# Seven normalisations of a two-block transformer kernel: statistics with tokens on partitions instead of tokens on columns

## The chip, the cores and the metric

The kernel runs on one core of one Trainium2 chip. TensorE (PE) multiplies matrices, VectorE (DVE) and ScalarE (ACT) do the elementwise work, and the DMA queues bring the weights. The metric is the device time of one execution in microseconds (us); shorter is better. The kernel before has a median of 2540.64 us over three runs (2532.92 to 2546.59).

## The reference, cut to what matters

Two blocks follow one another, each of two layers, on 256 tokens of width 1024 (the first block carries 256 context tokens beside them, so 512 columns up to its second layer). In front of and behind every mixer and feed-forward stage stands a norm. The first block has RMS norms, the second has layer norms:

```python
def rmsnorm(x, g):
    xf = x.astype(jnp.float32)
    y = xf * lax.rsqrt(jnp.mean(xf * xf, axis=-1, keepdims=True) + EPS)
    return (y * g.astype(jnp.float32)).astype(x.dtype)

def modulate(x, g, shift, scale):
    return rmsnorm(x, g) * (1 + scale) + shift
...
        x = layer_norm(DN_ALPHA * x + y, ln_g[layer, 0], ln_b[layer, 0])
        j = layer // 2
        if layer % 2 == 0:
            y = swiglu_2(x, ffn_w1[j], ffn_w3[j], ffn_w2[j])
        else:
            y = moe_ffn(x, router_w[j], router_b[j], exp_w1[j], exp_w3[j], exp_w2[j])
        x = layer_norm(DN_ALPHA * x + y, ln_g[layer, 1], ln_b[layer, 1])
```

Each norm needs one number per token, the reciprocal root of a mean over the 1024 features, and multiplies all features of the token by it. Everything is fp32 outside and inside.

## The kernel before, in words

The activations `X` lie with features on the 128 partitions, in 8 tiles (`KD = 8`), and tokens on the columns: `[128, 8, tt]` with `tt` = 512 (`TT`) or 256 (`T`). A mean over features is therefore a sum over partitions and over 8 tiles. The kernel takes it with PE: a product with the constant matrix `mean_d` (128 x 128, every entry 1/1024) sums over the partitions and at the same time leaves the sum on every partition. One fp32 product shows in the profile as two passes, each with a weight load (PEld) and a MATMUL record.

Every projection is a product of high and low parts: ACT writes the high part of an operand (`AH`, `PH`, `WH`), DVE the low part (`AL`, `PL`, `WL`), and PE runs three products for each tile. Six units of output take PSUM banks 0 to 5 in turn (`BANKS = 6`), bank 6 is `NORM` and bank 7 `MEAN`; bank 5 is also called `FIRST_NORM`. Each engine has its own instruction stream in the order of the code, and they meet by semaphores.

The norms are numbered by `ni`. Norm 0 is at the start. Norms 1 and 2 are RMS norms of 512 columns, norms 3 and 4 RMS norms of 256 columns, norms 5, 6 and 7 layer norms of 256 columns. The last layer norm of all is made in another way and has no part in this.

An RMS norm (1 to 4) runs as follows. While the stage before it puts out its last tiles, ACT squares `X` tile by tile into `SQ` and DVE adds the squares into `RS` (`summed`). Then PE multiplies `RS` by `mean_d` (L954), ACT takes the root of the whole `tt` columns (its record has the helper's line L1605), DVE takes the reciprocal of `RS` in place (L2040), and for each of the 8 feature tiles DVE multiplies `X` by gain and `RS` (L2050, one instruction for each 256 columns), ACT writes the high part and DVE the low part (L2062 or L2059). The next projection's first products (`split_group`, L837 to L841) wait for the low part of the first tile. In a layer norm DVE sums `X` instead of the squares, PE makes the mean (L950), DVE subtracts it (L2038), ACT squares, and PE accumulates 8 products of `mean_d` with the 8 square tiles (L943). Norm 7 is followed by the router's products (L1073), which write bank 6 in the kernel before.

In DVE's stream the reciprocal waits for the root, and everything behind it on DVE (the multiplications, the low parts, later weight chunks' low parts `WL`) is queued behind that wait. PE has nothing to issue between L954 (or L943) and the first product of the next stage.

Of the kernel before, what the change touches and what calls it, by code (L numbers as in the profile page):

```python
# [21 lines left out]
ALU = mybir.AluOpType  # L22
# [3 lines left out]
P = 128  # L26
D = 1024
# [295 lines left out]
def build(nc, stream, experts, params, consts, xin, final_rows, out):  # L323
    with ExitStack() as ctx:
# [3 lines left out]
        def sem(name):  # L328
            return ctx.enter_context(nc.semaphore(name))
# [92 lines left out]
        def cn(name, a=0, b=None):  # L422
            lo, hi = CO[name]
            return con[:, lo + a:(hi if b is None else lo + b)]
# [11 lines left out]
        def small(at, n):  # L436
            return smalls[:, at:at + n]
# [15 lines left out]
        nsink = small(24, 32)  # L453
        lam = small(60, 8)
        cs = small(177, 8 * KD + 6)

        Q0, K0, U0, VG, VV = (view(2048 * n, 4, TT) for n in range(5))
        CAT0 = view(10240, KD, TT)
# [120 lines left out]
        n_sq, n_mm, n_root, n_x, n_a = sem("norm_sq"), sem("norm_mm"), sem("norm_root"), sem("norm_x"), sem("norm_a")  # L579
        n_mean, n_c, n_sum = sem("norm_mean"), sem("norm_centred"), sem("norm_sum")  # L580
        n_out = sem("norm_written")
        dve_chain, act_chain = sem("dve_chain"), sem("act_chain")
        at_s, at_m, at_e, at_n = sem("att_scores"), sem("att_max"), sem("att_exp"), sem("att_normed")
        at_t, at_tv, at_o, at_out = sem("att_turned"), sem("att_turned_copy"), sem("att_pv"), sem("att_out")
# [176 lines left out]
        def _(pe):  # L761
# [178 lines left out]
            def mean_square(ni, tt, j):  # L940

                pe.wait_ge(n_sq, KD * ni + j + 1)
                return pe.matmul((NORM if ni else FIRST_NORM)[:, 0:tt], cn("mean_d"), SQ[:, j, 0:tt],  # L943
                                 start=j == 0, stop=j == KD - 1)

            def norm_end(ni, tt):

                pe.wait_ge(n_sum, (KD - 1) * ni)
                if ni >= 5:
                    pe.matmul(MEAN[:, 0:tt], cn("mean_d"), RS[:, 0:tt], start=True, stop=True).then_inc(n_mean, 1)  # L950
                    for j in range(KD):
                        ins = mean_square(ni, tt, j)
                else:
                    ins = pe.matmul(NORM[:, 0:tt], cn("mean_d"), RS[:, 0:tt], start=True, stop=True)  # L954
                ins.then_inc(n_mm, 1)

            def attention(us, kind, early, late=None):

# [106 lines left out]
            def dispatch():  # L1065

                pe.wait_ge(gemm_free, st["u"])
                pe.wait_ge(route_tables, 2)
                pe.matmul(bank[5][:, 0:P], ONES[:, :], BEFORE[:, :], start=True, stop=True).then_inc(slot_mm, 1)
                rw = pr("router_w").rearrange("p (k e) -> p k e", k=KD)  # L1070
                for kk in range(KD):
                    pe.wait_ge(n_out, 2 * KD + kk + 1)
                    ins = pe.matmul(bank[6][0:EXPERTS, 0:T], rw[:, kk, :], X[:, kk, 0:T], start=kk == 0, stop=kk == KD - 1)  # L1073
                ins.then_inc(router_mm, 1)

                def turn_x(t, dh):

                    for c in range(4):
                        ins = pe.transpose(bank[2 + 2 * t + dh][:, c * P:(c + 1) * P], X[:, 4 * dh + c, t * P:(t + 1) * P], ident)
                    ins.then_inc(x_turned, 1)  # L1080

                turn_x(0, 0)
                pe.wait_ge(router_kept, 1)
                for t in range(2):
                    ins = pe.transpose(bank[7][:, 8 * t:8 * t + 8], LGT[0:8, t * P:(t + 1) * P], ident[0:8, 0:8])
                ins.then_inc(router_turned, 1)
                turn_x(0, 1)
                turn_x(1, 0)
                pe.wait_ge(slot_kept, 1)
                turn_x(1, 1)  # L1090

                pe.wait_ge(mask_ready, 1)
                for t in range(2):
                    ins = pe.matmul(bank[6][:, 0:EXPERTS], ONES[:, :], MASK[:, t, :], start=t == 0, stop=t == 1)
                ins.then_inc(count_mm, 1)
                pe.wait_ge(ranks_ready, 1)
                pe.matmul(bank[6][:, 0:16], BEFORE[:, :], MASK[:, :, :].rearrange("p a b -> p (a b)"), start=True, stop=True)
                pe.matmul(bank[6][:, 16:24], ONES[:, :], MASK[:, 0, :], start=True, stop=True).then_inc(place_mm, 1)
# [502 lines left out]
        def _(act):  # L1601
# [27 lines left out]
            def norm_root(ni, tt, eps):  # L1629

                act.wait_ge(n_mm, ni + 1)
                f(RS[:, 0:tt], (NORM if ni else FIRST_NORM)[:, 0:tt], ACT.Sqrt, bias=eps).then_inc(n_root, 1)

            def norm_written(ni, tt, high, bias):
# [354 lines left out]
        def _(dve):  # L1989
# [44 lines left out]
            def norm(ni, tt, gain, shift, high, low, gains_of=None):  # L2034
                if ni >= 5:
                    dve.wait_ge(n_mean, ni - 4)
                    for j in range(KD):
                        V.tensor_tensor(X[:, j, 0:tt], X[:, j, 0:tt], MEAN[:, 0:tt], ALU.subtract).then_inc(n_c, 1)  # L2038
                dve.wait_ge(n_root, ni + 1)
                link(V.reciprocal(RS[:, 0:tt], RS[:, 0:tt]))  # L2040
                if gains_of is not None:
                    gains_of()
                if ni >= 5:
                    dve.wait_ge(n_c, KD * (ni - 4))
                dst = X if shift is None else SQ
                for j in range(KD + 1):
                    if j < KD:
                        for s in range(tt // T):
                            cols = slice(s * T, (s + 1) * T)
                            ins = V.scalar_tensor_tensor(dst[:, j, cols], X[:, j, cols], gain(j, s), RS[:, cols],  # L2050
                                                         ALU.mult, ALU.mult)
                        ins.then_inc(n_x, 1)
                    if j and low is not None:

                        dve.wait_ge(n_a, KD * ni + j)
                        for s in range(tt // T):
                            cols = slice(s * T, (s + 1) * T)
                            if shift is None:
                                ins = V.tensor_tensor(low[:, j - 1, cols], X[:, j - 1, cols], high[:, j - 1, cols].bitcast(F32),  # L2059
                                                      ALU.subtract)  # L2060
                            else:
                                ins = V.scalar_tensor_tensor(low[:, j - 1, cols], SQ[:, j - 1, cols], shift(j - 1, s),  # L2062
                                                             high[:, j - 1, cols].bitcast(F32), ALU.add, ALU.subtract)
                        ins.then_inc(a_lo, 1)
# [172 lines left out]
            def choose():  # L2237

                dve.wait_ge(router_mm, 1)
                V.tensor_copy(LGT[0:8, :], bank[6][0:8, 0:T]).then_inc(router_kept, 1)  # L2240
                dve.wait_ge(router_turned, 1)
                for t in range(2):
                    ins = V.tensor_tensor(LG[:, 8 * t:8 * t + 8], bank[7][:, 8 * t:8 * t + 8], pr("router_b"), ALU.add)
# [629 lines left out]
    return out  # L2873


def tile_unit(j):

    return j if j < GROUP else 2 * j - GROUP
# [257 lines left out]
```

## Time and profile before

| what | value |
|---|---|
| median of three runs | 2540.64 us (2532.92 to 2546.59) |
| the profiled execution, its own time | 2548.69 us |
| its span, first to last instruction | 2546.9 us |
| PE busy | 95% of the span |
| DVE busy, ACT busy | 61%, 43% |
| mean granted TensorE clock | 0.978 of full speed |

A busy share says how long an engine had at least one instruction in work. The granted clock has two levels, full (2.4 GHz, shown as 1.00) and half (1.2 GHz, shown as 0.50); a stretch with a value between has some of each.

### The profile page before, as it was taken

What the parts mean: (1) busy time and instruction counts of PE and PEld (TensorE: products, weight loads), DVE (VectorE), ACT (ScalarE), POOL (GpSimd) and SP (SyncE); (2) the same over time, 40 slices, a digit from 0 to 9 for tenths busy, and PEclk for the clock granted to TensorE, in tenths of its full rate; (3) what the DMA queues carried; (4) which work ended last, traced back from release to release, by engine and by line L of the source; (5) the groups of instructions that cost most, each with busy time, mean ns of one, the idle gap of its engine ahead of it and who ended that gap; (6) DMA issues with size and microseconds to landing.
All of it is one profiled execution on the core that took longest, in us unless ns stands there. A gap on an engine that the chain in (4) does not pass through costs nothing.

```text
span 2546.9 us, 39512 instructions
## 1 busy us (share of the span) xinstructions
PE 2419.7 (95%) x14953; PEld 2015.4 (79%) x14953; DVE 1540.9 (61%) x3333; ACT 1082.6 (43%) x1972; POOL 0.2 (0%) x4
## 2 busy tenths in 40 slices
PE   7998889999898899999999899899998899999998
PEld 3853678888684799997797899897897688878885
DVE  3567553333477765657675666656756655558893
ACT  3236333223226554543402545542303454557882
POOL 0000000000000000000000000000000000000000
PEclk8999999999999999999999999999999899999999
DMA  8348422333224566553323466443322565459997
GB/s 325 96 148 285 144 83 93 98 97 94 82 83 152 174 192 183 167 170 100 95 76 113 153 199 195 148 131 97 103 75 75 205 186 178 133 200 349 330 356 278
DMA packets 182492, 410.08 MB, mean 161 GB/s; under 512 B 20256, under 2 KB 20512, under 8 KB 181792
## 3 DMA queue, kind: packets, MB, share of 16 engines
q1 hardware_dynamic: 182304, 407.56, 49.0%
q8 instruction: 120, 1.97, 0.3%
q14 instruction: 68, 0.56, 0.1%
HBM read 406.43 MB, written 1.05 MB: 160 GB/s over the span
## 4 chain that ended last, share of the span: by engine, by line
PE 88%; DVE 8%; ACT 1%; issue 1%; DMA 1%; SPq 0%; DVEq 0%; ACTq 0%
PE bank L817 11%; PE bank L821 11%; PE bank L820 11%; PE bank L1042 8%; PE bank L1059 5%; PE bank L1062 5%; PE bank L1063 5%; PE bank L779 5%; PE bank L837 3%; PE bank L840 3%; PE bank L841 3%; PE bank L906 2%; PE bank L969 2%; PE bank L1017 2%; PE bank L1194 1%
## 5 line engine op out<-in xcount | busy, mean ns | idle before, releaser
L2222 DVE TENSOR_TENSOR WL<-ring,WH 128x512 fp32r<-128x512 f32 x632 | 412.2, 688 | 251.9 <-ACT WH L1605 250.6
L1605 ACT ACTIVATE WH<-ring 128x512 fp32r<-128x512 f32 x632 | 375.4, 625 | 299.4 <-PE bank L817 204.1
L2307 DVE TENSOR_TENSOR WLE<-slots,WHE 128x1024 fp32r<-128x1024 f32 x231 | 281.4, 1224 | 122.9 <-ACT WHE L1605 119.5
L1605 ACT ACTIVATE WHE<-slots 128x1024 fp32r<-128x1024 f32 x231 | 244.7, 1061 | 114.4 <-PE bank L1059 112.9
L817 PE MATMUL bank<-AH,WH 128*128 128x256 f32 (+1 forms) x864 | 274.1, 317 | 1.0 <-DVE WL L2222 1.0
L821 PE MATMUL bank<-AH,WL 128*128 128x256 f32 (+1 forms) x864 | 273.4, 316 | 0.0
L820 PE MATMUL bank<-AL,WH 128*128 128x256 f32 (+1 forms) x864 | 272.2, 315 | 0.0
L1042 PE MATMUL bank<-X,ring 128*128 128x256 f32 x1024 | 248.1, 389 | 5.4 <-ACT A L1605 5.4
L1042 PEld LDWEIGHTS bank<-X,ring 128*128 128x128 f32 x1024 | 189.8, 192 | 40.8 <-issue 7.6
L821 PEld LDWEIGHTS bank<-AH,WL 128*128 128x128 f32 x864 | 163.4, 189 | 12.7
L817 PEld LDWEIGHTS bank<-AH,WH 128*128 128x128 f32 x864 | 162.3, 188 | 11.9 <-issue 1.2
L820 PEld LDWEIGHTS bank<-AL,WH 128*128 128x128 f32 x864 | 162.2, 188 | 12.1
L817 PE MATMUL bank<-HH,WH 128*128 128x256 f32 (+1 forms) x528 | 167.4, 317 | 0.0
L821 PE MATMUL bank<-HH,WL 128*128 128x256 f32 (+1 forms) x528 | 167.0, 316 | 0.0
L820 PE MATMUL bank<-HL,WH 128*128 128x256 f32 (+1 forms) x528 | 166.3, 315 | 0.0
L1059 PE MATMUL bank<-WHE,XEH 128*128 128x512 f32 (+1 forms) x432 | 164.1, 380 | 0.2 <-DVE WLE L2307 0.2
L1063 PE MATMUL bank<-WLE,XEH 128*128 128x512 f32 (+1 forms) x432 | 160.9, 372 | 0.0
L1062 PE MATMUL bank<-WHE,XEL 128*128 128x512 f32 (+1 forms) x432 | 160.7, 372 | 0.0
L817 PE MATMUL bank<-PH,WH 128*128 128x256 f32 (+2 forms) x480 | 146.1, 304 | 0.0
L821 PE MATMUL bank<-PH,WL 128*128 128x256 f32 (+2 forms) x480 | 143.7, 299 | 0.0
L820 PE MATMUL bank<-PL,WH 128*128 128x256 f32 (+2 forms) x416 | 122.2, 294 | 0.0
L1605 ACT ACTIVATE A<-bank,par 128x256 f32<-128x256 f32 x60 | 28.3, 471 | 221.1 <-PE bank L1042 192.3
(345 smaller groups left out, 4782.9 us busy)
## 6 DMA issues: line engine op xcount, KB each, us to landing
ring<-stream SPq DMA_DIRECT2D x992, 256.0 KB, 2.8
slots<-experts SPq DMA_DIRECT2D x264, 512.0 KB, 5.1
con<-consts SPq DMA_DIRECT2D x1, 3204.0 KB, 12.9
X<-xin SPq DMA_DIRECT2D x1, 2048.0 KB, 10.1
par<-params SPq DMA_DIRECT2D x1, 1302.5 KB, 5.8
LAST<-final_rows SPq DMA_DIRECT2D x1, 1024.0 KB, 4.8
out<-ZO SPq DMA_DIRECT2D x4, 256.0 KB, 2.0
con<-consts SPq DMA_DIRECT2D x1, 132.0 KB, 2.7
```

Of the source, the lines that this page charges most:

```text
L779: ins = pe.matmul(o, l, r, start=start, stop=stop)
L817: ins = pe.matmul(o, wh, hi(kk), start=kk == 0, stop=False)
L820: read_signal(pe.matmul(o, wh, lo(kk), start=False, stop=False))
L821: ins = pe.matmul(o, wl, hi(kk), start=False, stop=kk == k - 1)
L837: ins = pe.matmul(o, wh, hi(kk, tt), start=kk == 0, stop=False)
L1042: ins = pe.matmul(o, weight(st["n"]), X[:, kk, 0:T], start=kk == 0, stop=kk == KD - 1)
L1059: ins = pe.matmul(o, hi, WHE[:, s, at:at + w], start=start, stop=False)
L1062: pe.matmul(o, lo, WHE[:, s, at:at + w], start=False, stop=False)
L1063: return pe.matmul(o, hi, WLE[:, s, at:at + w], start=False, stop=stop)
L1605: return nc.scalar.activation(o, i, fn, **kw)
L2222: V.tensor_tensor(WL[:, s % SPLIT, :], ring[:, c % RING, :], WH[:, s % SPLIT, :].bitcast(F32), ALU.subtract).then_inc(w_taken, 1)
L2307: V.tensor_tensor(WLE[:, s % PAIR_SPLIT, :], pair(pair_of(s)), WHE[:, s % PAIR_SPLIT, :].bitcast(F32), ALU.subtract).then_inc(pair_taken, 1)
```

## The change

The statistics are kept with tokens on partitions. For norms 1 to 4, PE takes 128 tokens of `RS` as the stationary operand and one column of `mean_d` as the moving one; the product is one column of 128 mean squares, one product for each 128 tokens. For norms 5 to 7 the same is done for each of the 8 square tiles, with two accumulators in banks 6 and 5 (16 products in place of 8). ACT takes the root of these few columns into `token_root`, DVE takes their reciprocal, and then, for each 128 tokens, DVE multiplies the identity matrix by them and by 1024 (a diagonal matrix in `RS`), and PE multiplies that by `mean_d`, which spreads each token's number over all partitions, into bank 6. DVE's multiplications then read bank 6 instead of `RS`. The router's product goes to bank 1, since bank 6 is still being read. Norm 0 and the means of the layer norms are as they were.

```diff
@@ def norm_end(ni, tt) on PE
                 if ni >= 5:
                     pe.matmul(MEAN[:, 0:tt], cn("mean_d"), RS[:, 0:tt], start=True, stop=True).then_inc(n_mean, 1)
                     for j in range(KD):
-                        ins = mean_square(ni, tt, j)
+                        pe.wait_ge(n_sq, KD * ni + j + 1)
+                        for t, o in enumerate((NORM, FIRST_NORM)):
+                            ins = pe.matmul(o[:, 0:1], SQ[:, j, t * P:(t + 1) * P], cn("mean_d", 0, 1), start=j == 0, stop=j == KD - 1)
                 else:
-                    ins = pe.matmul(NORM[:, 0:tt], cn("mean_d"), RS[:, 0:tt], start=True, stop=True)
+                    for t in range(tt // P):
+                        ins = pe.matmul(NORM[:, t:t + 1], RS[:, t * P:(t + 1) * P], cn("mean_d", 0, 1), start=True, stop=True)
                 ins.then_inc(n_mm, 1)
+                if ni:
+
+                    for t in range(tt // P):
+                        pe.wait_ge(n_spread, spread_before(ni) + t + 1)
+                        ins = pe.matmul(NORM[:, t * P:(t + 1) * P], cn("mean_d"), RS[:, t * P:(t + 1) * P], start=True, stop=True)
+                        if t == tt // P - 1:
+                            ins.then_inc(n_back, 1)
@@ router on PE
-                    ins = pe.matmul(bank[6][0:EXPERTS, 0:T], rw[:, kk, :], X[:, kk, 0:T], start=kk == 0, stop=kk == KD - 1)
+                    ins = pe.matmul(bank[1][0:EXPERTS, 0:T], rw[:, kk, :], X[:, kk, 0:T], start=kk == 0, stop=kk == KD - 1)
@@ def norm_root(ni, tt, eps) on ACT
                 act.wait_ge(n_mm, ni + 1)
+                if ni >= 5:
+                    f(token_root[:, 0:1], NORM[:, 0:1], ACT.Sqrt, bias=eps)
+                    f(token_root[:, 1:2], FIRST_NORM[:, 0:1], ACT.Sqrt, bias=eps).then_inc(n_root, 1)
+                    return
+                if ni:
+                    f(token_root[:, 0:tt // P], NORM[:, 0:tt // P], ACT.Sqrt, bias=eps).then_inc(n_root, 1)
+                    return
@@ def norm(ni, tt, ...) on DVE
                 dve.wait_ge(n_root, ni + 1)
-                link(V.reciprocal(RS[:, 0:tt], RS[:, 0:tt]))
+                if ni:
+
+                    link(V.reciprocal(token_root[:, 0:tt // P], token_root[:, 0:tt // P]))
+                    for t in range(tt // P):
+                        V.tensor_scalar(RS[:, t * P:(t + 1) * P], ident, token_root[:, t:t + 1], float(D),
+                                        ALU.mult, ALU.mult).then_inc(n_spread, 1)
+                    root = NORM
+                else:
+                    link(V.reciprocal(RS[:, 0:tt], RS[:, 0:tt]))
+                    root = RS
...
-                            ins = V.scalar_tensor_tensor(dst[:, j, cols], X[:, j, cols], gain(j, s), RS[:, cols],
+                            if j == 0 and ni:
+                                dve.wait_ge(n_back, ni)
+                            ins = V.scalar_tensor_tensor(dst[:, j, cols], X[:, j, cols], gain(j, s), root[:, cols],
                                                          ALU.mult, ALU.mult)
```

How the instructions stand is shown at two places. The first is PE at norm 5, the layer norm behind the second block's first mixer. The rows are PE's products in order, `bank` is the output in PSUM, and of the operands `con` is the constant `mean_d`; the last of `w_out_2`'s projection stands ahead, the first product of the feed-forward stage behind. Before:

```order
L820 MATMUL bank<-CL,WH 128x256
L821 MATMUL bank<-PL,WL 128x256
L950 MATMUL bank<-RS,con 128x256
L943 MATMUL bank<-SQ,con 128x256 x8
L837 MATMUL bank<-AH,WH 128x256
```

and in the changed kernel:

```order
L822 MATMUL bank<-CL,WH 128x256
L823 MATMUL bank<-PL,WL 128x256
L952 MATMUL bank<-RS,con 128x256
L956 MATMUL bank<-con,SQ 128x1 x16
L965 MATMUL bank<-RS,con 128x128 x2
L839 MATMUL bank<-AH,WH 128x256
```

Eight products of 256 columns have become sixteen of one column, and two products of 128 columns stand between them and the feed-forward stage.

The second place is DVE at norm 1, the RMS norm of 512 columns in front of the first feed-forward stage; L2506 is the residual of the last tile and L2077 the sum of the squares. Before:

```order
L2506 SCALAR_TENSOR_TENSOR X<-bank3,mod,X 128x256 x2
L2077 TENSOR_TENSOR RS<-RS,SQ 128x512 x2
L2040 RECIPROCAL RS<-RS 128x512
L2050 SCALAR_TENSOR_TENSOR SQ<-X,modg,RS 128x256 x4
L2062 SCALAR_TENSOR_TENSOR AL<-SQ,mod,AH 128x256 x2
```

and in the changed kernel:

```order
L2536 SCALAR_TENSOR_TENSOR X<-bank3,mod,X 128x256 x2
L2107 TENSOR_TENSOR RS<-RS,SQ 128x512 x2
L2061 RECIPROCAL smalls<-smalls 128x4
L2063 TENSOR_SCALAR RS<-con,smalls 128x128 x4
L2080 SCALAR_TENSOR_TENSOR SQ<-X,modg,bank6 128x256 x4
L2092 SCALAR_TENSOR_TENSOR AL<-SQ,mod,AH 128x256 x2
```

One reciprocal of 512 columns has become one of 4 columns and four scalings of the identity, and the first multiplication behind them waits for PE's spreading products.

## Rows read from the trace of the kernel before

**Rows 1.** The page: busy time, and the chain that ended last.

```profile
PE 2419.7 (95%) x14953; PEld 2015.4 (79%) x14953; DVE 1540.9 (61%) x3333; ACT 1082.6 (43%) x1972; POOL 0.2 (0%) x4
...
PE 88%; DVE 8%; ACT 1%; issue 1%; DMA 1%; SPq 0%; DVEq 0%; ACTq 0%
```

**Rows 2.** Timeline at norm 1: start, duration, engine, line [idle before, releaser].

```profile
315.52 2.05 PE L954 MATMUL bank<-RS,con 128*128 128x512 f32 x2 [2.36 <-DVE RS L2077]
317.60 0.69 ACT L1605 ACTIVATE RS<-bank,par 128x512 f32<-128x512 f32 x1 [2.87 <-PE bank L954]
318.39 3.35 DVE L2040 RECIPROCAL RS<-RS 128x512 f32<-128x512 f32 x1 [2.93 <-ACT RS L1605]
321.78 1.67 DVE L2050 SCALAR_TENSOR_TENSOR SQ<-X,modg,RS 128x256 f32<-128x256 f32 x4
...
324.77 0.77 PE L837 MATMUL bank<-AH,WH 128*128 128x512 f32 x1 [7.20 <-DVE AL L2062]
```

**Rows 3.** Timeline at norm 3, an RMS norm of 256 columns.

```profile
866.63 0.70 PE L954 MATMUL bank<-RS,con 128*128 128x256 f32 x2 [2.06 <-DVE RS L2077]
...
869.73 0.88 DVE L2050 SCALAR_TENSOR_TENSOR SQ<-X,modg,RS 128x256 f32<-128x256 f32 x2
...
871.53 0.55 PE L837 MATMUL bank<-AH,WH 128*128 128x256 f32 x1 [4.20 <-DVE AL L2062]
```

**Rows 4.** Timeline at norm 5, a layer norm.

```profile
1414.30 0.70 PE L950 MATMUL bank<-RS,con 128*128 128x256 f32 x2 [1.38 <-DVE RS L2077]
...
1416.03 3.72 PE L943 MATMUL bank<-SQ,con 128*128 128x256 f32 x16 [1.03 <-ACT SQ L1605]
1419.79 0.47 ACT L1605 ACTIVATE RS<-bank,par 128x256 f32<-128x256 f32 x1 [1.49 <-PE bank L943]
...
1422.08 0.88 DVE L2050 SCALAR_TENSOR_TENSOR SQ<-X,par,RS 128x256 f32<-128x256 f32 x2
...
1423.88 0.35 PE L837 MATMUL bank<-AH,WH 128*128 128x256 f32 x1 [4.13 <-DVE AL L2062]
```

**Rows 5.** Timeline at norm 2 and at norm 7, PE's mean-square products.

```profile
692.02 1.12 PE L954 MATMUL bank<-RS,con 128*128 128x512 f32 x2 [2.36 <-DVE RS L2077]
...
1970.10 5.41 PE L943 MATMUL bank<-SQ,con 128*128 128x256 f32 x16 [1.03 <-ACT SQ L1605]
```

**Rows 6.** Timeline elsewhere: small instructions like those that the change adds.

```profile
2010.73 0.52 PEld L1149 LDWEIGHTS bank<-S,PICK 128*128 128x128 f32 x4
2010.83 0.50 PE L1149 MATMUL bank<-S,PICK 128*128 128x1 f32 x4
...
2537.87 0.29 ACT L1605 ACTIVATE ROOT<-MOMENTS,par 128x1 f32<-128x1 f32 x1 [1.08 <-DVE MOMENTS L2440]
...
2540.07 0.16 DVE L2450 RECIPROCAL ROOT<-ROOT 128x2 f32<-128x2 f32 x1
2540.26 1.42 DVE L2455 SCALAR_TENSOR_TENSOR ZO<-ZO,ROOT,LAST 128x512 f32<-128x512 f32 x2
...
1992.17 0.48 DVE L2295 TENSOR_SCALAR PICK<-SLOT,PLACE 128x128 fp32r<-128x128 f32 x2
```

**Rows 7.** Groups by line and shape on DVE: count, busy, mean ns.

```profile
L2506 DVE SCALAR_TENSOR_TENSOR X<-bank,mod,X 128x256 f32<-128x256 f32 x72 | 32.2, 480 | 62.8 <-PE bank L821 60.8 <-PE bank L841 2.0
```

**Rows 8.** Windows: length, busy, PEclk, DMA; the sum of seven stretches at 0.50.

```profile
313.20:315.40 2.20, 0.00 (x0) 0.00 (x0) 2.10 (x4) 0.63 (x1) 0.00 (x0) 1.00 0.06 20
315.40:318.00 2.60, 2.05 (x2) 0.47 (x2) 0.07 (x1) 0.40 (x1) 0.00 (x0) 0.53 0.00 0
324.70:329.20 4.50, 4.43 (x11) 3.50 (x12) 4.50 (x13) 2.50 (x6) 0.00 (x0) 0.50 0.00 0
...
1416.00:1419.80 3.80, 3.72 (x16) 2.95 (x16) 1.84 (x6) 2.31 (x8) 0.00 (x0) 1.00 0.00 0
1419.80:1423.80 4.00, 0.00 (x0) 0.00 (x0) 3.29 (x5) 1.37 (x3) 0.00 (x0) 1.00 0.00 0
...
sum 29.60, PE 29.32 PEld 24.42 DVE 26.86 ACT 17.58 POOL 0.00; mean PE 4.19 PEld 3.49 DVE 3.84 ACT 2.51 POOL 0.00
```

More of the change, by code:

```diff
@@ L455, in build @@
         cs = small(177, 8 * KD + 6)
+        token_root = small(252, 4)
         Q0, K0, U0, VG, VV = (view(2048 * n, 4, TT) for n in range(5))
@@ L581, in build @@
         n_out = sem("norm_written")
+        n_spread, n_back = sem("norm_spread"), sem("norm_back")
         dve_chain, act_chain = sem("dve_chain"), sem("act_chain")
@@ L2239, in choose @@
                 dve.wait_ge(router_mm, 1)
-                V.tensor_copy(LGT[0:8, :], bank[6][0:8, 0:T]).then_inc(router_kept, 1)
+                V.tensor_copy(LGT[0:8, :], bank[1][0:8, 0:T]).then_inc(router_kept, 1)
                 dve.wait_ge(router_turned, 1)
@@ L2873, in _unit_bases, with spread_before @@
     return out
+def spread_before(ni):
+    return sum(TT // P if n < 3 else T // P for n in range(1, ni))
 def tile_unit(j):
```

## The prediction

> **What bounds the kernel now.** I read the page first: PE is busy for 95% of the span and makes up 88% of the chain that ended last [rows 1]. The reader is to see that only time in which PE stands still, or runs at half clock, can be won by work on DVE and ACT. Then I read the timeline at the norms, because each of them is such a place. At norm 1, PE's product with `mean_d` ends at 317.57 us (315.52 + 2.05) and PE's next product starts at 324.77 us, and the row says what it waited for: the low part on DVE. Between them stand one after another ACT's root (0.69), DVE's reciprocal (3.35) and from 321.78 us on the multiplications and the splitting into high and low parts [rows 2]. Nothing else runs on these engines meanwhile, so a microsecond taken out of the chain root, reciprocal, first multiplication starts the next stage a microsecond sooner. The stages behind are bound by PE, so it isn't lost again. Norm 3 shows the same in 256 columns [rows 3], and norm 5 the form of the layer norms, where PE's 16 passes take 3.72 before the root [rows 4].
>
> I count each norm in two pieces: the products, from their wait's end to their own end, and what I call the turn, from there to the start of the first multiplication (L2050). What follows L2050 (2.99 us to the next stage's first product at norm 1, 1.80 at norm 3) is unchanged, if the multiplication costs as much from PSUM as from SBUF. L2506 is the same instruction with one operand in PSUM and takes 480 ns for 256 columns [rows 7]; two L2050 take 0.88, as two of these did, and four 1.67 [rows 2, 3]. So I take nothing for it.
>
> **The products.** A one-column fp32 product costs its weight loads. Four passes of that kind take 0.52 in loads, 0.11 from one to the next with 0.19 for the last, and from the first load's start to the last record's end 0.60 (2010.73 to 2011.33) [rows 6]. That is 0.60 for the two products of norms 3 and 4, against 0.70 now [rows 3]; 0.60 + 4 x 0.11 = 1.04 for the four of norms 1 and 2, against 1.12 at full clock [rows 5]; and 0.60 + 28 x 0.11 = 3.68 for the sixteen of a layer norm, against 3.72 [rows 4]. The weight load takes as long as 256 columns do, so this step saves under 0.1 in each norm. At half clock both double alike: 2.05 for the same row at norm 1 [rows 2].
>
> Here one rule of the Trainium skill would say otherwise. "TensorE: Matmul & The Clock Gate", section "Back-to-back issue gap", gives a floor of some 25 ns from one small matmul to the next. By it the four products would take some 0.6 less than the 1.04 above, and over all norms the kernel would win an estimated 4 to 5 us more. The loads in the trace stand 110 ns apart with a one-column product behind each, and I go by them.
>
> **The turn.** For 512 columns now: 321.78 - 317.57 = 4.21 [rows 2]. Changed, step by step: 0.03 to ACT; the root of 4 columns, 0.27 (0.69 for 512 and 0.47 for 256 columns give 0.25 and 0.84 ns a column [rows 2, 4]; a root of one column with its bias as a tensor shows 0.29 [rows 6]); 0.10 to DVE; the reciprocal 0.16 and its link 0.03 (2540.07 to 2540.26) [rows 6]; the first scaled identity, 0.28 (two take 0.48, so they follow at 0.20) [rows 6]; 0.05 to PE; the spreading products; 0.10 back to DVE. The spreading products of four tiles have 8 passes of 128 columns, as many columns as the two passes of 512 of L954, so 1.12 at full clock [rows 5] and 2.05 at half [rows 2]. The identities come as fast as PE takes them. Sum 0.03 + 0.27 + 0.10 + 0.19 + 0.28 + 0.05 + 1.12 + 0.10 = 2.14, gain 2.07, with the products 2.15. At half clock 3.07, gain 1.2.
>
> For 256 columns now: 869.73 - 867.33 = 2.40 [rows 3]. Changed: the same with 0.70 for the spreading, 1.72, gain 0.68, with the products 0.78. At half clock the spreading takes 0.34 + 0.85 = 1.19 and 0.3 is left. In a layer norm now: 1422.08 - 1419.75 = 2.33 [rows 4]. Changed: 1.72 and 0.20 for a second root instruction (bank 5), 1.92, gain 0.45 with the products; at half clock nothing.
>
> Which clock? At norm 1 it fell from 1.00 to 0.5 about when L954 started, after PE had stood for 2.4 us [rows 8], so norm 1 counts at half: 1.2. At norms 2 to 4 it fell somewhere in the gap, so I take the middle: 1.7, 0.55 and 0.55. At norm 5 it was still full when the gap ended at 1423.8 [rows 8], so the three layer norms count in full: 3 x 0.45 = 1.35.
>
> **The sum.** 1.2 + 1.7 + 0.55 + 0.55 + 1.35 = 5.35 us. Everything at half clock gives 1.2 + 1.2 + 0.3 + 0.3 = 3.0, everything at full 2 x 2.15 + 2 x 0.78 + 1.35 = 7.2. Other edits are counted at nothing: the router's bank 1 is free by then, norm 0 is untouched, and DVE's stream behind the norm moves up as a whole. The profiled execution took 2548.69, 1.8 us around its span of 2546.9; that is 0.3% above the median of 2540.64. The sum is small enough to take it off either: 2548.7 - 5.4 = 2543.3 for a like execution, and 2540.6 - 5.4 = **2535.3** for the median. A measurement of this kernel can tell about 0.5%, 12.7 us, from no change; the three runs alone lie 13.7 us apart.
>
> **The rivals.** *The clock falls during the one-column products.* In a layer norm PE now streams 256 columns in every pass and the clock stays at 1.00 throughout and 4 us beyond [rows 8]. Afterwards nearly all of that time goes into loads with one column behind each. If the chip sees this as standing still, PE has had next to no work since the projection's end at 1412.9 (1414.30 - 1.38) [rows 4], and by norm 1's row the clock can fall 2.4 us after that [rows 8]. Then 28 passes at 0.22 instead of 0.11 cost 3.1 more in norms 5 and 6 and 1.5 in norm 7, where the products take 5.41 already, at half clock for most of it [rows 5]; the spreading costs 0.45 more in each. Together 9 us of loss against 5.35 of gain: slower, 2544.6. It decides once the half clock takes hold within about the first half of the sixteen products. For it: the fall at norm 1. Against it: the loads keep PE's array occupied, and the trace has no long run of one-column products to say.
>
> *The clock no longer falls.* After each of the seven norms the next stage starts at half clock: 4.5 us at norm 1, and behind norm 7 it is the router's products. The seven stretches are 29.6 us long together; the first and their sum are shown [rows 8]. Spreading breaks PE's long stand of 7.2 us at norm 1 [rows 2] in two, the longer part 3.0. If that keeps the clock up, half of 29.6 is won too, 14.8, with 7.2 at full clock: 2518.6. Against it speaks that 2.4 us of standing were enough at norm 1 [rows 8]. The same page of the Trainium skill ("Part 1: The HAM clock gate") says that half rate is the default and that activity releases it; a few short products in the gap could count for either side, and its rule alone doesn't say which.
>
> *The gain is not there.* The wait for the way back through PE, or slower reads from PSUM, eat what the reciprocal gave, or the time moves somewhere else by chance of when the clock rises again (a stretch longer or shorter by 1 us costs half of that, seven times): 2540.
>
> **How the numbers follow.** The forecast has 0.56, the fall during the products 0.20, the clock that stays 0.07, no gain 0.17. The range holds the forecast with its bounds (2533.4 to 2537.6), the first and last rival, and the scatter of a median of runs that lie 0.5% apart, some 6 us on either side of these: 2526 to 2548. Faster by over 0.5% (under 2527.9) needs the clock that stays, or luck: 0.08. Slower by over 0.5% (over 2553.3) needs the fall and bad luck: 0.03. The rest, 0.89, is within.
>
> **What would show it.** In the changed kernel's profile the reciprocal should be one of 0.16 for 2 or 4 columns in place of one of 3.35 at norms 1 and 2 and about half of that elsewhere; the turn should take 2.1 to 3.1 at norms 1 and 2, 1.7 to 2.2 at norms 3 and 4, 1.9 to 2.4 in the layer norms; L2050's successor should still take 0.48 with bank 6 as its operand; the sixteen one-column products should take 3.7. The forecast is wrong if these take 5 to 7 (the clock fell in them), if the stretches at half clock behind the norms are gone or twice as long, or if the multiplications from bank 6 are longer than 0.5.

## The result: slower by 0.34%, outside the forecast

| | before | changed |
|---|---|---|
| median of 16 runs each, us | 2545.37 (2532.92 to 2553.85) | 2556.09 (2544.01 to 2567.77) |
| profiled execution, us | 2548.69, span 2546.9 | 2562.82, span 2561.1 |
| mean granted clock of PE | 0.978 | 0.973 |

The ratio is 1.0034 with an interval of 1.0020 to 1.0048: the change costs 8.7 us (5 to 12), where 5.35 us of gain were forecast. The two medians lie further apart, 10.7 us; here and below the recorded ratios are used, which are not quotients of medians. Of the 20.8 us between the forecast of 2535.3 and the 2556.09 measured, 4.7 us are the kernel before, whose median rose from 2540.64 in three runs to 2545.37 in sixteen. One run of e2 (8401 us) and one of e3 (12783 us), kernels of the experiments below, were far slower than all others and count in no ratio and no mean clock.

The page of the changed kernel shows it as little as that of before did [rows 1]: PE has 26 us more of busy time, in 100 more instructions.

```profile
PE 2445.6 (95%) x15053; PEld 2038.1 (80%) x15053; DVE 1530.0 (60%) x3351; ACT 1081.0 (42%) x1975; POOL 0.2 (0%) x4
...
PE 89%; DVE 7%; DMA 2%; ACT 1%; issue 1%; SPq 0%; DVEq 0%; ACTq 0%
```

So the norms have to be read one by one. The timeline at norm 1, against [rows 2] (start, duration, engine, line):

```profile
317.28 1.54 PE L959 MATMUL bank<-con,RS 128*128 128x1 f32 x8 [2.36 <-DVE RS L2107]
318.86 0.26 ACT L1617 ACTIVATE smalls<-bank,par 128x4 f32<-128x4 f32 x1 [2.37 <-PE bank L959]
319.23 0.18 DVE L2061 RECIPROCAL smalls<-smalls 128x4 f32<-128x4 f32 x1 [2.00 <-ACT smalls L1617]
319.44 0.87 DVE L2063 TENSOR_SCALAR RS<-con,smalls 128x128 f32<-128x128 f32 x4
...
319.78 2.07 PE L965 MATMUL bank<-RS,con 128*128 128x128 f32 x8 [0.96 <-DVE RS L2063]
321.89 1.66 DVE L2080 SCALAR_TENSOR_TENSOR SQ<-X,modg,bank 128x256 f32<-128x256 f32 x4 [1.58 <-PE bank L965]
...
324.88 0.77 PE L839 MATMUL bank<-AH,WH 128*128 128x512 f32 x1 [3.02 <-DVE AL L2092]
```

The reader is to see that the turn, from the products' end at 318.82 to the first multiplication at 321.89, now takes 3.07 where it took 4.21. Norm 3, against [rows 3]:

```profile
871.70 0.61 PE L959 MATMUL bank<-con,RS 128*128 128x1 f32 x4 [1.59 <-DVE RS L2107]
...
873.25 0.71 PE L965 MATMUL bank<-RS,con 128*128 128x128 f32 x4 [0.94 <-DVE RS L2063]
874.00 0.87 DVE L2080 SCALAR_TENSOR_TENSOR SQ<-X,modg,bank 128x256 f32<-128x256 f32 x2 [0.61 <-PE bank L965]
...
875.79 0.55 PE L839 MATMUL bank<-AH,WH 128*128 128x256 f32 x1 [1.83 <-DVE AL L2092]
```

Here the turn is 874.00 - 872.31 = 1.69 instead of 2.40. The RMS norms gained. Norm 5, against [rows 4], is where it was lost:

```profile
1420.08 0.70 PE L952 MATMUL bank<-RS,con 128*128 128x256 f32 x2 [1.38 <-DVE RS L2107]
...
1421.81 5.39 PE L956 MATMUL bank<-con,SQ 128*128 128x1 f32 x32 [1.03 <-ACT SQ L1617]
1427.24 0.41 ACT L1617 ACTIVATE smalls<-bank,par 128x1 f32<-128x1 f32 x2 [3.17 <-PE bank L956]
...
1428.22 1.23 PE L965 MATMUL bank<-RS,con 128*128 128x128 f32 x4 [1.02 <-DVE RS L2063]
1429.57 0.87 DVE L2080 SCALAR_TENSOR_TENSOR SQ<-X,par,bank 128x256 f32<-128x256 f32 x2 [1.20 <-PE bank L965]
...
1431.36 0.55 PE L839 MATMUL bank<-AH,WH 128*128 128x256 f32 x1 [1.91 <-DVE AL L2092]
```

The one-column products take 5.39 instead of 3.72, the spreading 1.23 instead of 0.70. The windows at this place say why (length, busy of PE, its loads, DVE, ACT and POOL, then the granted clock). The first lies inside the products, the second too, the third behind the restart:

```profile
1421.80:1423.40 1.60, 1.59 (x15) 1.59 (x15) 1.60 (x6) 1.60 (x6) 0.00 (x0) 1.00 0.00 0
1423.60:1427.20 3.60, 3.60 (x18) 3.51 (x17) 0.02 (x1) 0.47 (x2) 0.00 (x0) 0.50 0.00 0
...
1431.30:1437.20 5.90, 5.84 (x27) 5.87 (x28) 5.61 (x14) 4.27 (x9) 0.00 (x0) 0.50 0.02 4
```

PE is busy without a break, products and loads, and in the middle of that, between 1423.4 and 1423.6 us, the clock goes from 1.00 to 0.50 (from 2.4 to 1.2 GHz): 15 passes in 1.6 us, then 18 in 3.6. Before, it was 1.00 during the products and 4 us beyond [rows 8]. The other two layer norms, from PE's timeline of the changed kernel:

```profile
1618.60 6.99 PE L956 MATMUL bank<-con,SQ 128*128 128x1 f32 x32 [1.03 <-ACT SQ L1617]
...
1982.81 6.50 PE L956 MATMUL bank<-con,SQ 128*128 128x1 f32 x32 [1.03 <-ACT SQ L1617]
```

At norm 6 the whole row runs at half clock. But there the clock fell before the first one-column product, which starts at 1618.60. The windows from the mean product on:

```profile
1616.80:1618.10 1.30, 0.70 (x2) 0.30 (x2) 0.44 (x3) 0.00 (x0) 0.00 (x0) 1.00 0.00 0
1618.20:1618.60 0.40, 0.00 (x1) 0.00 (x1) 0.40 (x2) 0.40 (x2) 0.00 (x0) 0.50 0.00 0
...
1618.20:1635.20 17.00, 13.67 (x61) 13.32 (x62) 9.43 (x26) 7.87 (x21) 0.00 (x0) 0.50 0.00 1
```

So the one-column products can't have brought this fall about; what they can have done is keep the clock down, for 17 us. At norm 7 it fell inside them, some 0.6 us behind their start.

To add this up I read, for each norm, two lengths off PE's records: the gap (start of the last product ahead of the norm to start of the first of the next stage) and the stretch (the same and the next 110 records, which takes in the half clock behind the norm). In us, one profiled execution each, for all kernels of this study (the next section says what e1 to e11 are). Beside them stand the mean granted clock over all runs of the kernel and the measured ratio; "again" is a second execution of the kernel before:

| kernel | gaps 1-4 | gaps 5-7 | stretches 1-4 | stretches 5-7 | mean clock | ratio (interval) |
|---|---|---|---|---|---|---|
| before | 36.8 | 31.1 | 114.6 | 95.0 | 0.979 | |
| before, again | 36.3 | 29.4 | 114.6 | 90.0 | 0.980 (one run) | |
| changed | 31.9 | 39.4 | 110.6 | 101.4 | 0.974 | 1.0034 (1.0020-1.0048) |
| e1 RMS norms only | 31.8 | 32.4 | 111.2 | 95.4 | 0.978 | 0.9997 (0.9979-1.0016) |
| e2 layer norms only | 36.3 | 39.6 | 116.1 | 101.3 | 0.974 | 1.0021 (1.0005-1.0037) |
| e3 128 columns, layer norms | 32.7 | 33.5 | 109.3 | 92.1 | 0.979 | 0.9979 (0.9956-1.0003) |
| e7 128 columns, all norms | 32.7 | 32.2 | 111.4 | 89.9 | 0.980 | 0.9973 (0.9949-0.9996) |
| e5 = e3 + idle products | 39.4 | 38.7 | 111.0 | 96.0 | 0.988 | 1.0008 (0.9990-1.0025) |
| e6 before + idle products | 53.8 | 44.7 | 124.9 | 97.7 | 0.988 | 1.0054 (1.0031-1.0076) |
| e8 changed + idle products | 39.4 | 45.4 | 111.0 | 100.6 | 0.986 | 1.0036 (1.0013-1.0060) |
| e9 = e7 + fitted idle products | 30.4 | 32.3 | 105.4 | 90.2 | 0.988 | 0.9970 (0.9952-0.9988) |
| e10 before + fitted | 35.9 | 33.3 | 109.5 | 91.8 | 0.987 | 0.9985 (0.9968-1.0002) |
| e11 changed + fitted | 30.0 | 38.5 | 104.8 | 96.0 | 0.983 | 0.9990 (0.9972-1.0008) |

The change shortens the stretches of norms 1 to 4 by 4.0 us and lengthens those of norms 5 to 7 by 6.4 (by 11.4 against the other execution of before). That is 2.4 to 7.4 us of the 8.7. The two profiled spans lie 14.2 us apart; 6.3 of that is between norms 1 and 2, where the change does nothing, and the last section shows what it is; the rest is spread over the start, the other stages and the end, up to 2 us in each.

The clock speaks for more than one execution. In the 16 runs of the changed kernel it was 0.971 to 0.976, in the 91 runs of the kernel before that were made beside the experiments 0.976 to 0.983. Of the kernels without idle products, the two with one-column products in the layer norms, the changed one and e2, have 0.974, and e1, e3 and e7 have 0.978 to 0.980. A clock lower by 0.0055 over 2550 us takes some 14 us of full speed, an estimate from above, since half clock costs nothing where PE stands. The change lost 8.7 us net of the 4 to 5 us that the RMS norms gain in the traces, which leaves little for any other cause.

### The profile page after: what moved, and what is told of

It is laid out like the page before. It is cut to its first block, busy times and chain, and to the rows that moved or that the text cites. A ratio compares the mean times of both kernels' runs of the same rounds, so it can differ in the third digit from the quotient of the medians.

```text
span 2561.1 us, 39733 instructions
## 1 busy us (share of the span) xinstructions
PE 2445.6 (95%) x15053; PEld 2038.1 (80%) x15053; DVE 1530.0 (60%) x3351; ACT 1081.0 (42%) x1975; POOL 0.2 (0%) x4
## 4 chain that ended last, share of the span: by engine, by line
PE 89%; DVE 7%; DMA 2%; ACT 1%; issue 1%; SPq 0%; DVEq 0%; ACTq 0%
PE bank L819 11%; PE bank L822 11%; PE bank L823 11%; PE bank L1054 9%; PE bank L781 6%; PE bank L1071 5%; PE bank L1075 5%; PE bank L1074 5%; PE bank L839 3%; PE bank L842 3%; PE bank L843 3%; PE bank L981 2%; PE bank L1029 2%; PE bank L908 2%; PE bank L1206 1%; DMA ring<-stream 1%
## 6 DMA issues: line engine op xcount, KB each, us to landing
X<-xin SPq DMA_DIRECT2D x1, 2048.0 KB, 10.1
```

## The experiments

The theory after the result was the prediction's own first rival: PE's clock falls in the layer norms because the products stream one column each. The rivals to it were that the RMS norms or the way back through PE cost it, that the number of loads (32 passes where there were 16) does, or that it comes from the scatter of single executions. All medians below are of 10 to 12 runs, but for e4, and each ratio is against runs of the kernel before on the same chip.

**e1 and e2: one half of the change each.** e1 keeps the new way for norms 1 to 4, e2 for norms 5 to 7.

The diff is e1's, on PE, ACT and DVE; in e2 the last condition reads `ni >= 5`, and norms 1 to 4 go as before.

```diff
-                        pe.wait_ge(n_sq, KD * ni + j + 1)
-                        for t, o in enumerate((NORM, FIRST_NORM)):
-                            ins = pe.matmul(o[:, 0:1], SQ[:, j, t * P:(t + 1) * P], cn("mean_d", 0, 1), start=j == 0, stop=j == KD - 1)
+                        ins = mean_square(ni, tt, j)
...
-                if ni:
+                if 0 < ni < 5:
```

> Norms 1 to 4 as in the changed kernel, norms 5 to 7 with the products of 256 columns, roots and reciprocals of the kernel before (the router's bank stays 1). Theory A (the loss is the half clock that the one-column products of the layer norms bring, and the RMS norms gain): the gaps of norms 1 to 4 are shorter by 4 to 5 us in sum as in the changed kernel, norms 5 to 7 as before, and the time is 4 to 5 us under before (0.998). Rival B (a loss that the whole change brings somewhere in the dense stages, such as products 233 ns apart instead of 229 between norms 1 and 2): the time is above before by 4 us or more although the gaps are shorter. Rival C (nothing but scatter): within 2 us of before.

> Norms 5 to 7 as in the changed kernel, norms 1 to 4 as before. Theory A: the one-column products take 5.4 or more in norms 5 and 6 in place of 3.72, the half clock lasts 10 us or more around each, the three gaps with the 110 products behind each are 6 us longer in sum, and the time is 6 to 12 us above before. Rival B: products 233 ns apart again between norms 1 and 2 only if these norms are changed, so not here, and a time within 3 us of before. Rival C: within 2 us of before.

Measured: e1 2547.23 us, ratio 0.9997, e2 2555.92 us, ratio 1.0021. The RMS norms bring 0.8 us (5 of gain to 4 of loss by the interval; the stretches of the trace say 3.4 of gain), the layer norms cost 5.3 us (1 to 9; the stretches say 6.3). The loss sits in the layer norms (the 4 to 5 us of gain expected of e1 lie within its interval, and so does nothing at all). PE's timeline of e2 has the fall at norm 5 again:

```profile
1426.53 5.68 PE L956 MATMUL bank<-con,SQ 128*128 128x1 f32 x32 [1.03 <-ACT SQ L1616]
```

But e1 held something that neither theory had foreseen. Its mean-square products at norm 6 are those of before, with 256 columns in every pass, and took

```profile
1609.46 6.72 PE L945 MATMUL bank<-SQ,con 128*128 128x256 f32 x16 [1.03 <-ACT SQ L1615]
```

against 3.72 at norms 5 and 7 of the same execution. The clock had fallen 0.7 us ahead of these products. So it can fall without one-column products, as norm 7 of the kernel before had already shown [rows 5]. e1's stretch at norm 6 is 30.9 us long and the changed kernel's 31.1, against 27.6 before. So of the 6.4 us that its trace shows lost in norms 5 to 7, the changed kernel lost 3.5 here, behind a fall that one-column products didn't start, and e1 lost 3.3 here with the old products.

**e3: the same loads, 128 columns behind each.** Only the width of the moving operand and of the output differ from the changed kernel.

```diff
-ins = pe.matmul(o[:, 0:1], SQ[:, j, t * P:(t + 1) * P], cn("mean_d", 0, 1), ...)
+ins = pe.matmul(o[:, 0:128], SQ[:, j, t * P:(t + 1) * P], cn("mean_d", 0, 128), ...)
```

> The changed kernel, but each of the sixteen mean-square products of a layer norm streams 128 columns of the constant instead of one (the same weight loads, the same 16 products; the 127 further columns aren't read). Theory A (the clock follows the columns streamed): the clock stays full through these products, they take 3.7 to 4.0, the half clock behind the norms is 3.4 to 7 as before, and the time falls 6 to 10 us under the changed kernel's, to some 4 us under before. Rival D (the clock falls since PE waits more or the loads are slow, whatever is streamed): still 5.4 or more for the products and the changed kernel's time.

Measured: 2544.94 us, ratio 0.9979. Against the changed kernel's 1.0034 that is 0.55%, 14 us (some 7 to 21 with both intervals), and the stretches are 10.6 us shorter together. PE's timeline of e3 at norms 5 and 6:

```profile
1403.45 3.84 PE L956 MATMUL bank<-con,SQ 128*128 128x128 f32 x32 [1.03 <-ACT SQ L1617]
...
1603.39 6.75 PE L956 MATMUL bank<-con,SQ 128*128 128x128 f32 x32 [1.03 <-ACT SQ L1617]
```

and its windows at norm 5, the products and the turn behind them:

```profile
1403.40:1407.40 4.00, 3.84 (x32) 3.65 (x32) 1.86 (x6) 2.39 (x8) 0.00 (x0) 1.00 0.00 0
1407.40:1411.40 4.00, 1.18 (x8) 1.02 (x9) 2.72 (x9) 1.53 (x5) 0.00 (x0) 1.00 0.00 0
```

The 32 loads are the same, and with 127 more columns in each they take 3.84, where one-column products at full clock take 3.73 (e11 below). At norm 5 the clock is 1.00 in the products and past them. The number of loads is out as a cause, and so is the way back through PE: both stayed. What PE streams in these passes decides most of it. At norm 6 the clock fell ahead of the products as in e1, so width doesn't prevent every fall. The windows there, the half clock and what follows it:

```profile
1602.80:1609.50 6.70, 6.11 (x28) 6.11 (x29) 2.41 (x8) 2.73 (x8) 0.00 (x0) 0.50 0.00 0
1609.60:1612.90 3.30, 1.26 (x9) 0.87 (x8) 1.52 (x5) 0.80 (x3) 0.00 (x0) 1.00 0.00 0
```

With 128 columns the clock was full again after 6.8 us, near the end of the products (in e1 too), and fell once more behind them. With one column, from the same start, it stayed at half for 17 us in the changed kernel and in e2. Against the 6 to 10 us that were expected the gain is 14, and its interval of 7 to 21 allows both.

**e4: the kernel before once more**, for the scatter of its trace.

> The kernel before once more, for a second profile. In its first profile the products of 512 columns between norms 1 and 2 started 228.9 ns apart, in the changed kernel's 233.3, and those of 256 columns 113.3 in some stages and 117.8 in others. If that spacing is a matter of the execution and not of the program, some stage shows the other value here (theory C for that part of the difference, 6.3 us); if it belongs to the program, every stage shows what it showed.

Measured: 2540.44 us in one execution. Between norms 3 and 4 the spacing was 113.3 ns where the first trace had 117.8, so there it is a matter of the execution; between norms 1 and 2 it was 228.9 again. All three layer norms kept full clock in their products and their stretches are 5.0 us shorter than in the first trace of before, which shows how much one trace's number for a stretch is worth.

Counted over the executions without idle products: one-column products ran at half clock in part or in whole at 6 of 6 layer norms (the changed kernel and e2), products with 128 or 256 columns at 4 of 15 (norm 7 of before, norm 6 of e1 and e3, norm 5 of e7). Norm 6 of the changed kernel, e1, e2 and e3 fell ahead of the products, whatever their width. Of those that began at full clock, the one-column products lost it at 4 of 4 norms and the wider ones at 2 of 13.

**e7: 128 columns in the RMS norms too.** e3's edit, and the products of norms 1 to 4 widened likewise.

```diff
-ins = pe.matmul(NORM[:, t:t + 1], RS[:, t * P:(t + 1) * P], cn("mean_d", 0, 1), ...)
+ins = pe.matmul(NORM[:, t * P:(t + 1) * P], RS[:, t * P:(t + 1) * P], cn("mean_d"), ...)
```

> As the kernel with 128 columns in the layer norms, and 128 columns also in the mean-square products of norms 1 to 4 (the same loads; one column of each is read). Theory A: norms 1 to 4 had only four or eight such passes, about 1 us, so the time is within 3 us of the kernel with 128 columns in the layer norms alone.

Measured: 2539.11 us, ratio 0.9973. The same as e3 within the intervals; gaps 1 to 4 are the same to 0.04. The norms' few passes with one column cost nothing that shows. This version is 0.27% faster than the kernel before (0.0 to 0.5%) and 0.6% faster than the changed one.

**e5, e6, e8: can the clock be held up by idle work?** To test the rival by which the clock no longer falls, products whose result nobody reads were put into PE's waits: ahead of the mean product, behind it, behind the one-column products and behind the spreading (e5 in e3, e8 in the changed kernel, e6 in the kernel before).

```diff
+def fill(o, n):
+    for _ in range(n):
+        pe.matmul(o[:, 0:512], cn("mean_d"), con[:, 0:512], start=True, stop=True)
...
+fill(NORM, 4 if tt == TT else 2)      # ahead of the norm's first wait
...
+fill(NORM, 2)                         # behind a layer norm's mean product
...
+fill(bank[0], 2)                      # behind the mean-square products (e6: 15, or 9 for 256 tokens)
...
+fill(bank[0], 6 if tt == TT else 4)   # behind the spreading (e6 has none)
```

> The changed kernel with 128 columns in each mean-square product of the layer norms, and with products that nobody reads (512 columns of constants, 0.43 us each at full clock) wherever PE stands in a norm: 4 or 2 ahead of the sum, 2 behind the mean, 2 ahead of the spreading and 6 or 4 behind it. Theory A (what PE streams keeps the clock up, and half clock behind the norms costs about half its length): the clock stays full through the norms, the half clock outside the kernel's first 60 us falls from some 80 us to under 40, and the time is 10 to 16 us under before (0.994 to 0.996). Rival E (the clock falls at these places whatever PE does, or the idle products delay the real ones as much as they save): within 4 us of the kernel with 128 columns and without them.

> The kernel before with the same kind of products that nobody reads: 4 or 2 ahead of the sum, 2 behind the mean, 15 or 9 between the mean squares and the next stage. Theory A: full clock through the norms and behind them, 8 to 12 us under before, since nothing of the chain on DVE is shorter. Rival E: within 3 us of before, or slower, if the products delay the next stage.

> The changed kernel with its one-column products, and the idle products of the second kernel of this set around them. Theory A (columns streamed count over a stretch): idle products stand ahead of and behind the sixteen one-column products but not among them, so the clock falls in them less often or later, the three layer norms lose less, and the time is 8 to 16 us under the changed kernel's. If a run of one-column products lowers the clock by itself, whatever stands around it, they take 5.4 again in norms 5 and 6 and the time is only 4 to 8 us under the changed kernel's, from norms 1 to 4.

Measured: ratios 1.0008, 1.0054 and 1.0036, so none of the three gains came. The expectations sized an idle product at half of what it takes: an fp32 product of 512 columns is two passes of 0.43, so the idle products outlasted the waits that they were to fill. e5's gap at norm 1 is 11.9 us where e3's is 10.1 (it restarted at 323.87 instead of 322.57), and e6's gaps are 30.5 us longer than before's in all. The mean granted clock rose to 0.988, 0.988 and 0.986. The half clock, counted from 60 us on and without the drop at the kernel's very end, fell to 41.0, 47.8 and 51.2 us, from 88.7 before (81.9 in its second execution, 112.6 in the changed kernel). These three runs say that idle products hold the clock, and say nothing yet of what that is worth.

e5 and e8 differ only in the width of the layer norms' products, and this is the cleanest comparison of one column with 128, since PE has work all through the norm. The windows at norm 6, from the first of these products to the restart, of e5:

```profile
1608.52:1617.29 8.77, 8.77 (x49) 6.14 (x48) 4.51 (x14) 3.58 (x11) 0.00 (x0) 1.00 0.00 0
```

and of e8:

```profile
1605.15:1617.25 12.10, 12.10 (x49) 8.31 (x48) 4.66 (x14) 3.72 (x12) 0.00 (x0) 0.72 0.00 0
```

In e8 the clock fell among these products at norm 6 (4.60 us). At norms 5 and 7 they kept full clock to their end (3.63 us each), and it fell 0.1 and 1.2 us behind them, among the idle products. So with one column the clock fell in all three layer norms, with 128 in none. By the ratios the difference is 0.28%, 7 us, with an interval from nothing to 15.

**e9, e10, e11: the same with idle products that fit**: 256 columns each, 5 (3 for 256 tokens) ahead, 2, 2, and 6 (4) behind; e9 in e7, e10 in the kernel before (16 and 9 behind the mean squares), e11 in the changed kernel.

> The idle products of the earlier kernels were twice as long as I had taken them for: an fp32 product of 512 columns is two passes, 0.85 us, and with them the next stage after norm 1 began at 323.9 instead of 322.6. Here they are of 256 columns, 0.43 each, 5 or 3 ahead of the sum, 2 behind the mean, 2 ahead of the spreading, 6 or 4 behind it, on the kernel with 128 columns in all mean-square products. Theory A (half clock costs half its length, and idle products that fit into PE's standing cost nothing): gaps as in that kernel within 0.5 us each, half clock outside the first 60 us under 45 us in place of 80, and 10 to 15 us under before (0.994 to 0.996), which beats both kernels. Rival F (the clock isn't worth that, or the idle products still delay): within 3 us of the kernel with 128 columns in all (0.9973).

> The kernel before with idle products of 256 columns: 5 or 3 ahead of the sum, 2 behind the mean, 16 or 9 between the mean squares and the next stage. Theory A: full clock behind the norms, gaps as before within 0.7 us each, 6 to 12 us under before. Rival F: within 3 us of before.

> The changed kernel (one column in its products) with the idle products of the first kernel of this set. Theory A: the clock falls now and then among or just behind the sixteen one-column products, less than in the changed kernel; 6 to 12 us under the changed kernel, that is within 4 us of before. If it is 10 us or more under before, the one-column products do no harm once PE is busy around them.

Measured: e9 2537.19 us, ratio 0.9970, e10 2541.22, 0.9985, e11 2542.72, 0.9990. PE's timeline of e9 at norm 1, idle products being L951:

```profile
312.28 2.32 PE L951 MATMUL bank<-con 128*128 128x256 f32 x10
314.80 1.16 PE L966 MATMUL bank<-con,RS 128*128 128x128 f32 x8 [0.20 <-DVE RS L2116]
315.79 1.03 PE L951 MATMUL bank<-con 128*128 128x256 f32 x4
316.92 1.16 PE L973 MATMUL bank<-RS,con 128*128 128x128 f32 x8
317.91 2.76 PE L951 MATMUL bank<-con 128*128 128x256 f32 x12
321.09 0.47 PE L839 MATMUL bank<-AH,WH 128*128 128x512 f32 x1 [0.42 <-DVE AL L2101]
```

and its window behind the restart, where [rows 8] has 0.50:

```profile
321.00:325.50 4.50, 4.41 (x19) 3.68 (x20) 4.50 (x13) 2.51 (x6) 0.00 (x0) 1.00 0.02 4
```

The spreading takes 1.16 instead of 2.07 and the next stage starts at full clock. In e11 the clock in the one-column products held longer. PE's timeline of e11 at norm 5:

```profile
1409.63 3.73 PE L963 MATMUL bank<-con,SQ 128*128 128x1 f32 x32 [0.17 <-ACT SQ L1626]
```

At norms 6 and 7 of e11 the same row took 4.64 and 5.00; at norm 5 the clock fell 1.1 us behind it. Counted over all kernels with idle products, the clock fell between the first mean-square product and the restart at 6 of 6 layer norms with one-column products (e8, e11) and at 0 of 12 with wider ones (e5, e6, e9, e10). e11 against the changed kernel is 0.44%, 11 us, as its stretches say (212.0 to 200.9): the rescue of a loss. On the kernel before the same filling brings 0.15%, not told from nothing. On e7 it brings 0.03% by the ratios, though e9's stretches are 5.7 us shorter than e7's; at that size the ratios don't tell. So of the expectations e11's was met and those of e9 and e10 were not: 7.6 us (3 to 12) and 4 us under before, not 10 to 15 and 6 to 12, and e9 lies within the 3 us of e7 that rival F allowed.

## Why the prediction was wrong

**The products of norms 1 to 4** took 0.61 at norm 3 (forecast 0.60), 0.11 from load to load. The Trainium skill's floor of some 25 ns ("TensorE: Matmul & The Clock Gate", "Back-to-back issue gap") was no rival to this: the same section says that in a stream of loads and products both set the spacing, and the 0.11 us agree with that. The forecast was right to go by the loads.

**The turn** took 3.07 at norm 1 (forecast 3.07 at half clock) and 1.69 at norm 3 (forecast 1.72). The reciprocal fell to 0.18. The multiplication costs no more from bank 6 than from SBUF, as the groups by shape on DVE show beside L2506 [rows 7]:

```profile
L2080 DVE SCALAR_TENSOR_TENSOR SQ<-X,modg,bank 128x256 f32<-128x256 f32 x40 | 17.4, 472 | 3.8 <-PE bank L965 3.8
...
L2080 DVE SCALAR_TENSOR_TENSOR SQ<-X,modg,RS 128x256 f32<-128x256 f32 x16 | 6.9, 479 | 0.0
```

The gaps of norms 1 to 4 shrank by 5.0 where 4.0 was forecast, the stretches by 4.0. This part of the sum stands in the trace, and there the rival "the gain is not there" falls; e1's ratio alone, 0.9979 to 1.0016, would allow it.

**The step that failed** is the one in "Which clock?": "so the three layer norms count in full: 3 x 0.45 = 1.35". It read the clock of the old products at norm 5 and carried it over to new ones that stream one column, and to norms 6 and 7, though norm 7 of the kernel before was already at half clock in most of its products [rows 5]. What the runs showed in its place is the first rival, "the clock falls during the one-column products": 5.39, 6.99 and 6.50 in place of 3.7, the gaps 5 to 7 longer by 8.3 and the stretches by 6.4 to 11.4, where the rival had priced 9. Its mechanism was right, its price of the loss near, and its chance of 0.20 too small; its net loss of 4 us is below the 5 to 12 measured. Luck has a part too: at norm 6 the clock fell ahead of the one-column products, and the gap is longer by 3.3 us; in e1, with the old products, the same fall made it longer by 3.0. The argument held against it, "the loads keep PE's array occupied", is refuted by the windows of the changed kernel: loads fill 1.59 of the 1.60 us right before the fall and 3.51 of the 3.60 us behind it. The rival's own row for the fall, 2.4 us behind the projection's end, was early at norm 5: there it came 4.8 us behind it (1418.7 to 1423.5), after about half of the passes, just where the rival's condition ends; at norm 6 it came 2.7 us behind it. And the rival missed a part: the half clock behind the restart grew as well, to 5.9 us at norm 5 from 3.4.

One reading of the prediction was wrong without bearing on the sum: not all seven stages restart at half clock. At norms 5 and 7 of the kernel before the clock was still full at the restart and fell some 1.0 and 2.5 us behind it.

**"The clock no longer falls"** didn't happen by itself. e9 to e11 forced it, and it is worth some 4 us on the kernel before (e10: 8 us of gain to 0.5 of loss), not the 14.8 us that the rival had counted for the half clock behind the norms; e10 still had 51.2 us of half clock outside the start, so this doesn't bound what full clock everywhere would bring.

**What stays open.** Why the clock also falls at single layer norms with wide products, in one execution and not in another. The part of the 8.7 us beyond the stretches' 2.4 to 7.4 was not traced to a place, though the clock over all runs leaves room for it. e1's and e2's differences add to 4.5 us; their intervals, some 5 and 4 us wide to either side, cover 8.7.

## What to carry to other kernels

A small product isn't only short or long, it is also what keeps PE's clock up or lets it fall: where 32 weight loads follow each other, 128 columns behind each cost 0.11 us in all, kept a clock that was full on entry at 4 of 5 norms where one column lost it at 4 of 4, and were worth 0.55% of the kernel (e3 against the changed one). When a change replaces what an engine streams, the clock read from the old rows mustn't be carried over; give the fall the larger chance if a neighbouring row already shows half clock. Size idle products by a row of their own (here two passes each) before placing them.

## What the runs showed of the hardware

The pace of dense products takes one of two values, for a whole stage of one execution. The windows 400 to 640 us (512 columns) and 900 to 1040 us (256 columns) lie where PE never waits and the clock is 1.00. Before:

```profile
400.00:640.00 240.00, 240.00 (x1050) 196.95 (x1049) 87.61 (x156) 69.70 (x122) 0.00 (x0) 1.00 0.31 96
900.00:1040.00 140.00, 140.00 (x1191) 140.00 (x1191) 85.05 (x166) 71.33 (x139) 0.00 (x0) 1.00 0.60 188
```

Changed:

```profile
400.00:640.00 240.00, 240.00 (x1030) 194.38 (x1030) 85.90 (x152) 68.79 (x120) 0.00 (x0) 1.00 0.30 92
```

The kernel before, again (e4):

```profile
900.00:1040.00 140.00, 140.00 (x1238) 140.00 (x1237) 87.82 (x172) 73.85 (x145) 0.00 (x0) 1.00 0.63 194
```

240 us hold 1050 products in one and 1030 in the other: 229 and 233 ns each. 140 us hold 1191 or 1238: 117.5 and 113.1 ns, and that is one program in two executions, so for 256 columns it isn't the program. For 512 columns this isn't shown, since neither kernel with the longer value was profiled twice. Over all thirteen traces, 512 columns took the longer value between norms 1 and 2 in the changed kernel and e2 alone, which makes 6.3 us there (364.5 to 370.8 us between the two norms' gaps); 256 columns took it between norms 3 and 4 in eight traces. Some 4.4 ns a product in one stage of 1,473 records make about 6.5 us, so two or three such stages could by themselves put two runs of one kernel 15 us apart (an estimate), and a single trace's span says little of a change of 0.3%. What sets the value wasn't found.
